# One layer of a hybrid decoder on one core: the last down projection by thirds of tokens with the final LayerNorm between its steps, the copy of x made later, the latents read back from another queue

## The chip, the cores and the metric

The kernel runs on one core of a Trainium2 chip. The metric is the device time of one execution in microseconds (us), the median over several runs. TensorE does the matrix products, VectorE and ScalarE the elementwise work and the reads of PSUM, GpSimd further elementwise work and the issue of some transfers, SyncE only issues transfers.

## What is computed

1024 prompt tokens and 8 x 4 sample tokens (T = 1056 in all) pass one layer. Cut to what matters here:

```python
z = x @ w_in + b_in                      # GLU | q latent 384 | kv latent 256 | rope key 64 | gates
u = causal_dwconv(a * sigmoid(g));  y_conv = silu(layer_norm(u)) @ w_conv_out
c_kv = rms_norm(z_kv);  q = rms_norm(z_q) @ w_uq;  o = attention(q, c_kv, rope(z_kr))
mix = (sigmoid(gA) * y_conv + sigmoid(gB) * (o @ w_uv @ w_mla_out)) @ w_mix_out
x1 = layer_norm(alpha * x + mix)
h = causal_dwconv(x1 @ w_up);  f = (silu(hg) * hv) @ w_down        # D_FF = 2816
y = layer_norm(alpha * x1 + f) * g2 + b2
```

Besides y the kernel returns the new latents, the last rows of both convolutions (the state rows) and, of the sample group, the old convolution rows moved on by four.

## The kernel before

**Layout.** Channels lie on the 128 partitions and tokens along the free axis, so that a tile is 128 channels x 1056 tokens, held in three thirds of 352 columns (`CH`). All products are made in float32 precision out of parts: `w = whi + wlo`, `x = xh + xl`, and each 128 x 128 block of weights takes three matmuls per third (`product`, L2006). ScalarE makes the high part `whi` of each block of weights (`hi`, L680), GpSimd the low part `wlo` (`lo`, L1244); two raw buffers (`RAW`) are filled by SyncE's transfers and each is released by `lo`. Two accumulators in PSUM, `psa` and `psb` (the buffers `psx[0]` and `psx[1]`, of three banks each), take turns, and the semaphores `free[0]` and `free[1]` count their reads; `pst` has two more banks. Everything is ordered by hand: each engine has its own list of instructions, and semaphores tie the lists together.

**Start.** Nine tiles of 128 tokens (the ninth has 32) are loaded as rows, turned over on TensorE (L2032), and read from PSUM three or four times: ScalarE writes `xh` (L688), VectorE `xl` (L1388), the sum over channels `stat` (L1390) and a copy of x, `xst` (L1393), which GpSimd sends to DRAM as `xt_d` (L1238). The copy has two buffers. Then come the turned tables of vectors (L2036 to L2042), the column sums of x (L2020) and the turned state rows (L2054), and only then the first of 32 products with `w_in` (`in_products`).

**Latents.** The latents z are made at the end of the first stage, `kv0 kv1 kr q0 q1 q2`, and go to DRAM as `z_d` from ScalarE's queue. ScalarE then makes the last two swish tiles (L803, L806), of which VectorE takes the low part `sl` (L1497), which the product `ya0` waits for tile by tile. After the last `z_d` is out, ScalarE issues in this order the read of all six tiles into `zbuf` (L839), of the gates `gab[0]` and `gab[1]` (L841) and of the rope table `cs` (L842), waits for `zbuf`, and squares five tiles (L845). TensorE's order is `ya0`, `ya1` (products with `w_conv_out`), the column sums `skv` (two tiles) and `sq` (three), `ya2` to `ya7`. VectorE multiplies each `ya` by its gate (`merge_a`, L1510), which frees the accumulator, and inverts the roots of the sums (L1516, L1519).

**FFN and end.** Eleven groups of two 128-row blocks of the inner width run over the up product, the convolution and the down product; each down product of a group has eight output tiles of 1056 tokens, 18 matmuls each (L2546), and VectorE adds each to `res` (L1924). After the last group's eight tiles TensorE turns the state rows (L2572, 11 x 4 transposes), ScalarE copies them (L1215) and issues nine transfers (L1217, L1220), and then the final LayerNorm goes over nine tiles of tokens:

```python
for t in range(9):
    y_stats(t)        # L1971 two bn_stats from PSUM, L1975 aggregate, L1977 1/root, L1980 -mean/root
    if t:
        y_gain(t - 1) # L1986 times g2, after ScalarE's scaling of the tile (L1228)
y_gain(8)
```

GpSimd adds `b2` (L1375) and SyncE sends the rows out (L659); after the last, SyncE issues the copy of the old state rows from DRAM to DRAM (L662). The tile of turned `res` has two places in PSUM, so that TensorE (L2581) waits for ScalarE's read of the tile before the last.

## Time and profile before

| what | value |
|---|---|
| median of 3 runs | 2242.74 us (2235.79 to 2242.78) |
| the profiled execution, its own time | 2257.73 us |
| its span, first to last instruction | 2255.9 us |
| TensorE busy (matmul) | 2111.7 us, 94% |
| VectorE / ScalarE / GpSimd busy | 57% / 30% / 24% |
| mean granted TensorE clock | 0.97 of full speed |

The table is the page of the profiled execution. Times in the rows below count from the start of its span. "Idle before" of an instruction, in square brackets, is what its engine waited and for whom. The profiled execution is 15.0 us longer than the median of the runs.

### The profile page before, as it was taken

Reading aid. Unit: us, or ns where it says so; the run is one execution under the profiler, and the core shown is the slowest. Engines: PE = TensorE matmul, PEld = TensorE weight load, DVE = VectorE, ACT = ScalarE, POOL = GpSimd, SP = SyncE. Lnnn points to the kernel's source line nnn. Section 1 sums busy time; section 2 is a strip of 40 time slices with the busy share of each in tenths; the row PEclk is TensorE's granted clock in tenths of the full one; section 3 lists DMA queues with packets and bytes.
Section 4 is the critical chain, followed back from the end, with each engine's and each line's share of the span. In section 5 each row is a group of like instructions: output and inputs, shape, how many; then the busy total and the mean of one; then the engine's idle time right before and its main releaser. Section 6 shows DMA issues by size and latency. Waiting matters only on the chain.

```text
span 2255.9 us, 34989 instructions
## 1 busy us (share of the span) xinstructions
PE 2111.7 (94%) x13793; PEld 1998.2 (89%) x13793; DVE 1279.5 (57%) x1748; ACT 666.7 (30%) x1107; POOL 535.6 (24%) x281
## 2 busy tenths in 40 slices
PE   5999999998989999979988999999999999999993
PEld 4999999997979888866657999899999999999992
DVE  5799999943546666634333324855445454454545
ACT  2222222243224444433332112522222122222212
POOL 2213343302100000033320134522222222222213
PEclk9999999999989999979997999999999999999995
DMA  7222232215310000046542442111111111111102
GB/s 234 77 87 82 85 113 85 87 46 196 125 41 13 12 23 12 19 163 234 190 178 95 143 108 89 31 54 46 40 47 38 47 41 53 46 37 52 45 25 99
DMA packets 163557, 182.78 MB, mean 81 GB/s; under 512 B 19838, under 2 KB 136376, under 8 KB 159303
## 3 DMA queue, kind: packets, MB, share of 16 engines
q1 hardware_dynamic: 144101, 102.36, 15.3%
q0 software_dynamic: 8368, 46.27, 5.4%
q10 hardware_dynamic: 10979, 32.68, 3.8%
q8 instruction: 71, 1.16, 0.2%
q14 instruction: 38, 0.30, 0.0%
HBM read 150.21 MB, written 31.93 MB: 81 GB/s over the span
## 4 chain that ended last, share of the span: by engine, by line
PE 70%; issue 13%; DVE 8%; POOL 3%; ACT 2%; DMA 2%; ACTq 1%; POOLq 0%; DVEq 0%; SPq 0%
PE psa L2006 21%; PE psb L2006 20%; PE psb L2160 5%; PE psa L2160 4%; PE psa L2546 4%; PE psb L2546 4%; POOL wlo L1363 3%; PE psb L2386 1%; PE pst L2365 1%; PE psa L2333 1%; PE psb L2333 1%; PE pst L2230 1%; DVE ptl L1612 1%; DMA gab<-ga_d 1%; DMA xt_d<-xst 1%
## 5 line engine op out<-in xcount | busy, mean ns | idle before, releaser
L1363 POOL TENSOR_TENSOR wlo<-wraw,whi 128x1024 fp32r<-128x1024 f32 x64 | 173.1, 2718 | 565.1 <-ACT whi L1167 565.1
L1444 DVE SCALAR_TENSOR_TENSOR pst<-g_ext,wtap,pst 128x512 f32<-128x512 f32 x464 | 306.9, 750 | 0.0
L1244 POOL TENSOR_TENSOR wlo<-wraw,whi 128x1024 fp32r<-128x1024 f32 x64 | 154.1, 2416 | 446.5 <-ACT whi L680 303.8
L1892 DVE TENSOR_SCALAR hg<-ueg,fwv,vec 128x1024 f32<-128x1024 f32 x22 | 19.3, 875 | 239.7 <-ACT ueg L1192 232.1
L2006 PE MATMUL psa<-x1h,whi 128*128 128x352 f32 x504 | 109.9, 326 | 3.5 <-POOL wlo L1363 2.0
L2006 PE MATMUL psa<-x1l,whi 128*128 128x352 f32 x504 | 109.1, 325 | 0.0
L2006 PE MATMUL psa<-x1h,wlo 128*128 128x352 f32 x504 | 109.0, 324 | 0.0
L2006 PE MATMUL psb<-x1h,whi 128*128 128x352 f32 x504 | 109.0, 324 | 0.0
L2006 PE MATMUL psb<-x1h,wlo 128*128 128x352 f32 x504 | 108.6, 323 | 0.0
L2006 PE MATMUL psb<-x1l,whi 128*128 128x352 f32 x504 | 108.5, 323 | 0.0
L1895 DVE SCALAR_TENSOR_TENSOR hg<-ueg,fwv,hg 128x1024 f32<-128x1024 f32 x44 | 97.0, 2204 | 5.7 <-DVE hg L1895 0.2
L2006 PE MATMUL psa<-xh,whi 128*128 128x352 f32 x456 | 98.8, 325 | 1.1 <-ACT stat L771 1.1
L2006 PE MATMUL psa<-xh,wlo 128*128 128x352 f32 x456 | 98.3, 323 | 0.0
L2006 PE MATMUL psa<-xl,whi 128*128 128x352 f32 x456 | 98.2, 323 | 0.0
L2006 PE MATMUL psb<-xh,whi 128*128 128x352 f32 x432 | 93.5, 324 | 1.5 <-POOL wlo L1244 1.5
L1292 POOL TENSOR_TENSOR wlo<-wraw,whi 128x1024 fp32r<-128x1024 f32 (+1 forms) x16 | 25.3, 1606 | 292.9 <-ACT whi L862 292.9
L2006 PE MATMUL psb<-xh,wlo 128*128 128x352 f32 x432 | 93.1, 323 | 0.0
L2006 PE MATMUL psb<-xl,whi 128*128 128x352 f32 x432 | 93.0, 323 | 0.0
L1192 ACT ACTIVATE ueg<-psa 128x1056 f32<-128x1056 f32 x22 | 23.2, 1054 | 229.3 <-PE psa L2006 222.8
L2006 PEld LDWEIGHTS psa<-x1h,whi 128*128 128x128 f32 x504 | 86.4, 190 | 4.1 <-issue 4.1
L2006 PEld LDWEIGHTS psa<-x1h,wlo 128*128 128x128 f32 x504 | 86.9, 189 | 0.0
L2006 PEld LDWEIGHTS psb<-x1h,wlo 128*128 128x128 f32 x504 | 86.5, 188 | 0.0
(472 smaller groups left out, 5450.8 us busy)
## 6 DMA issues: line engine op xcount, KB each, us to landing
wraw<-in_w_up SPq DMA_DIRECT2D x44, 512.0 KB, 3.8
wraw<-in_w_in SPq DMA_DIRECT2D x37, 512.0 KB, 3.8
wraw<-in_w_down SPq DMA_DIRECT2D x22, 512.0 KB, 3.5
gb_d<-stg ACTq DMA_DIRECT2D x8, 528.0 KB, 2.6
ga_d<-stg ACTq DMA_DIRECT2D x8, 528.0 KB, 3.8
gab<-ga_d ACTq DMA_DIRECT2D x8, 528.0 KB, 5.0
ma_d<-stg ACTq DMA_DIRECT2D x8, 528.0 KB, 2.9
tmp<-gb_d SPq DMA_DIRECT2D x8, 528.0 KB, 3.7
```

The costliest lines, as they stand in the source:

```text
L1192: nc.scalar.activation(split(ue[v][:, FW - 1:]), acc(v), ACT.Copy).then_inc(free[v], 1)
L1244: nc.gpsimd.tensor_tensor(wlo[:, n % HL, :], wraw[:, n % RAW, :], whi[:, n % HL, :].bitcast(F32), ALU.subtract).then_inc(lo_done, 1)
L1292: nc.gpsimd.tensor_tensor(wlo[:, n % HL, 0:w], wraw[:, v, 0:w], whi[:, n % HL, 0:w].bitcast(F32), ALU.subtract).then_inc(lo_done, 1)
L1363: nc.gpsimd.tensor_tensor(wlo[:, (ns + 2) % HL, :], wraw[:, (ns + 2) % RAW, :], whi[:, (ns + 2) % HL, :].bitcast(F32), ALU.subtract).then_ ...
L1444: half[x] = link(nc.vector.scalar_tensor_tensor(out=dst, in0=src, scalar=tap(k_), in1=pst[:, x, :], op0=ALU.mult, op1=ALU.add))
L1612: nc.vector.tensor_tensor(ptl[:, 4 * g:4 * g + nb, cols], pst[:, (cum(q) + g) % 2, 0:nb * P].rearrange("p (k n) -> p k n", n=P), pth[:, 4 ...
L1895: nc.vector.scalar_tensor_tensor(out=h, in0=src, scalar=tap(k), in1=h, op0=ALU.mult, op1=ALU.add).then_inc(h_chain, 1)
L2006: last = nc.tensor.matmul(out[:, c, 0:CH], w[:, k, :], x[:, k, c * CH:(c + 1) * CH], start=(k == 0 and x is hi_x and w is wh), stop=(k == ...
L2160: r = nc.tensor.matmul(out, w, x, start=first and k == 0, stop=last and k == len(steps) - 1)
L2230: last = nc.tensor.transpose(pst[:, (cum(q) + g) % 2, (k % 4) * P:(k % 4 + 1) * P], pbuf[q % 3][:, k * P:(k + 1) * P], ident[:, :])
L2333: last = nc.tensor.transpose(dst[:, k, v * P:(v + 1) * P], cb[j][:, 4 * g + v, k * P:(k + 1) * P], ident[:, :])
L2546: last = nc.tensor.matmul(psx[q][:, c, 0:CH], w[:, k, cols], x[:, k, c * CH:(c + 1) * CH], start=k == 0 and w is wh and x is fh[p_], stop= ...
```

## The change

**Start.** The copy `xst` and its transfers go. GpSimd later makes each of the eight channel tiles of x again as `xh + xl` (`x_tile`) and sends it to `xt_d`, three after each group of four products. The first product is put ahead of the tables, the column sums and the state rows (`start_tables`), and the first block of weights is loaded ahead of the last x rows.

**Latents.** The read-back of `z_d`, `gab` and `cs` is issued by SyncE, in another order and in more pieces; `q2` is read from PSUM before the last two swish tiles; `ya2` goes ahead of the column sums; VectorE adds the squares first, so that each column sum takes one tile.

**End.** The last group's down product goes third by third (24 steps of six matmuls, four places in PSUM), the nine tiles of the LayerNorm are put between its steps and behind them, with four places in PSUM, GpSimd multiplies tiles 0, 2, 4 and 6 by `g2` itself, and the state rows go to the end, with one transfer for the sample rows instead of eight.

```diff
         for k, name in enumerate(("kv0", "kv1", "kr", "q0", "q1", "q2", "ya0", "ya1",
-                                  "skv", "sq", "ya2", "ya3", "ya4", "ya5", "ya6", "ya7")):
+                                  "ya2", "skv", "sq", "ya3", "ya4", "ya5", "ya6", "ya7")):
...
+        LAST_DN = 6 * (NG - 1)
+        ROWS_BY_GPSIMD = (0, 2, 4, 6)
+        YB = "ABABACDBC"
...
+        def y_half(t, n, h):
+            b = YB[t]
+            if b == "A":
+                return pst[0:n, h, :]
+            if b == "B":
+                return psx[h][0:n, 2, :]
+            return psx["CD".index(b)][0:n, h, :]
...
+        def last_acc(i):
+            return psx[i % 2][:, i // 2 % 2, 0:CH]
...
+                if t == 8:
+                    load(0, w_in_v[:, :, 0:P])
                 sp.wait_ge(x_hi, t - 3)
...
-            with sp.Fori(0, MT // 2) as i:
+            load(N1C, w_co_v[:, :, 0:P])
+            load(N1C + 1, w_co_v[:, :, P:2 * P])
+            sp.wait_ge(w_used, N1C + HL)
+            sp.wait_ge(stg_out[0], 16 * (MT + 4))
+            sp.dma_start(gab[0][:, :], ga_d[0]).then_inc(ga_in[0], 16)
+            sp.wait_ge(stg_out[1], 16 * (MT + 3))
+            sp.dma_start(zbuf[:, 0:5, :], z_d[0:5].rearrange("k p n -> p k n")).then_inc(z_in, 16)
+            sp.wait_ge(stg_out[1], 16 * (MT + 4))
+            sp.dma_start(gab[1][:, :], ga_d[1]).then_inc(ga_in[1], 16)
+            sp.dma_start(zbuf[:, 5, :], z_d[5]).then_inc(z_in, 16)
+            sp.dma_start(cs[:, :], A["c_rope"]).then_inc(cs_in, 16)
+            with sp.Fori(1, MT // 2) as i:
...
-            read_z("q2", 5, 1, V_Q + 2)
-
-
-            act.wait_ge(w_used, N1C + HL)
-            for j in range(2):
-                act.wait_ge(stg_out[j], 16 * (MT + 4))
-            act.dma_start(zbuf[:, :, :], z_d.rearrange("k p n -> p k n")).then_inc(z_in, 16)
-            for j in range(2):
-                act.dma_start(gab[j][:, :], ga_d[j]).then_inc(ga_in[j], 16)
-            act.dma_start(cs[:, :], A["c_rope"]).then_inc(cs_in, 16)
-            act.wait_ge(z_in, 16)
-            for k in range(5):
-                nc.scalar.activation(sqb[:, k, :], zbuf[:, k if k < 2 else k + 1, :], ACT.Square).then_inc(rms_sq, 1)
+                    read_z("q2", 5, 1, V_Q + 2)
+
...
             after_ya(0)
+            act.wait_ge(z_in, 32)
+            for k in range(5):
+                nc.scalar.activation(sqb[:, k, :], zbuf[:, k if k < 2 else k + 1, :], ACT.Square).then_inc(rms_sq, 1)
             after_ya(1)
+            after_ya(2)
             stat_read("skv", 2, rk[:, :], 1.0 / KL, RMS_EPS)
             stat_read("sq", 3, rq[:, :], 1.0 / QL, RMS_EPS)
-            after_ya(2)
             after_ya(3)
...
+            def state_copy(*rs):
+                for r in rs:
+                    act.wait_ge(kf_t, r + 1)
+                    nc.scalar.activation(fout[:, r * 512:(r + 1) * 512], pst[0:FK, r % 2, :], ACT.Copy).then_inc(kf_r, 1)
...
-                nc.scalar.activation(yrow[t % 4][0:n, :], psx[j][0:n, 0:2, :].rearrange("p b n -> p (b n)"),
-                                     ACT.Identity, scale=sd[j][0:n, 1:2], bias=mv[j][0:n, 0:1]).then_inc(y_n, 1)
+                for h in range(2):
+                    ins = nc.scalar.activation(yrow[t % 4][0:n, h * 512:(h + 1) * 512], y_half(t, n, h),
+                                               ACT.Identity, scale=sd[j][0:n, 1:2], bias=mv[j][0:n, 0:1])
+                ins.then_inc(y_n, 1)
+                state_copy(*{5: (0, 1), 6: (2, 3), 7: (4, 5, 6), 8: (7, 8, 9, 10)}.get(t, ()))
+            act.wait_ge(kf_r, FT // 2)
+            act.dma_start(O["ffn_p"][0, 0], fout[0:FW - 1, :]).then_inc(ffn_out, 16)
+            act.dma_start(O["ffn_s"][0].rearrange("b t c -> (b t) c"), fout[FW - 1:, :]).then_inc(ffn_out, 16)
...
-                n = P if t < 8 else NS
-                pool.wait_ge(free[t % 2], t // 2 + 2)
-                pool.dma_start(xt_d[:, :, t * P:t * P + n].rearrange("m p n -> p m n"), xst[t % 2][:, :, 0:n]
-                               ).then_inc(xt_out[t % 2], 16)
...
+            def x_tile(k):
+                if k >= 2:
+                    pool.wait_ge(xt_out[k % 2], 16 * (k // 2))
+                nc.gpsimd.tensor_tensor(tmp[k % 2][:, :], xh[:, k, :].bitcast(F32), xl[:, k, :].bitcast(F32), ALU.add
+                                        ).then_inc(x_sum, 1)
+                pool.wait_ge(x_sum, k + 1)
+                pool.dma_start(xt_d[k], tmp[k % 2][:, :]).then_inc(xt_out[k % 2], 16)
...
                 lo(4 * m)
                 lo(4 * m + 1)
+                if m == 0:
+                    pool.wait_ge(free[0], 6)
+                    pool.wait_ge(free[1], 5)
...
                 if m >= CSUM:
                     for k in ((0, 1) if m == CSUM else (m - 2,)):
                         centre(k)
-                lo(4 * m + 2)
-                lo(4 * m + 3)
+                for t in range(2):
+                    lo(4 * m + 2 + t)
+                    if m < CSUM:
+                        for k in range(3 * m, min(MT, 3 * m + 3)):
+                            if (k > 3 * m) == (t == 1):
+                                x_tile(k)
                 if m >= CSUM:
                     add_squares(max(1, m - 2))
...
-                pool.wait_ge(y_g, t + 1)
+                if t in ROWS_BY_GPSIMD:
+                    k = ROWS_BY_GPSIMD.index(t) + 1
+                    pool.wait_ge(y_n, t + 1)
+                    nc.gpsimd.tensor_tensor(yrow[t % 4][0:n, :], yrow[t % 4][0:n, :], g2[0:n, :], ALU.mult).then_inc(y_gp, 1)
+                    pool.wait_ge(y_gp, k)
+                else:
+                    pool.wait_ge(y_g, t - sum(v < t for v in ROWS_BY_GPSIMD) + 1)
                 nc.gpsimd.tensor_tensor(yrow[t % 4][0:n, :], yrow[t % 4][0:n, :], b2[0:n, :], ALU.add).then_inc(y_b, 1)
...
-                nc.vector.reduce_sum(stat[:, t * P:t * P + n], src.rearrange("p k n -> p n k"), axis=AX.X)
-                if t >= 2:
-                    dve.wait_ge(xt_out[t % 2], 16 * (t // 2))
-                nc.vector.tensor_copy(xst[t % 2][:, :, 0:n], src).then_inc(free[t % 2], 1)
+                nc.vector.reduce_sum(stat[:, t * P:t * P + n], src.rearrange("p k n -> p n k"), axis=AX.X
+                                     ).then_inc(free[t % 2], 1)
...
-            dve.wait_ge(xt_out[0], 16 * 5)
-            dve.wait_ge(xt_out[1], 16 * 4)
...
+            for a, b in ((0, 1), (2, 3)):
+                dve.wait_ge(rms_sq, b + 1)
+                nc.vector.tensor_tensor(sqb[:, a, :], sqb[:, a, :], sqb[:, b, :], ALU.add).then_inc(rms_add, 1)
+            dve.wait_ge(rms_sq, 5)
+            dve.wait_ge(rms_add, 2)
+            nc.vector.tensor_tensor(sqb[:, 2, :], sqb[:, 2, :], sqb[:, 4, :], ALU.add).then_inc(rms_add, 1)
+            merge_a(2)
             ready("skv")
             nc.vector.reciprocal(rk[:, :], rk[:, :]).then_inc(rms_c, 1)
-            merge_a(2)
...
+            def last_add(*steps):
+                for i in steps:
+                    c, m = divmod(i, MT)
+                    dve.wait_ge(dn_done, LAST_DN + i + 1)
+                    nc.vector.tensor_tensor(res[:, m, part3(c)], res[:, m, part3(c)], last_acc(i), ALU.add).then_inc(dl_add, 1)
...
-            for t in range(9):
-                y_stats(t)
-                if t:
-                    y_gain(t - 1)
+            last_add(*range(10))
+            y_stats(0)
+            last_add(10, 11)
+            y_scale(0)
+            last_add(12)
+            y_stats(1)
+            last_add(13)
+            y_scale(1)
+            last_add(14, 15, 16)
+            y_gain(1)
+            last_add(17)
+            y_stats(2)
+            last_add(18)
+            y_scale(2)
+            last_add(19, 20)
+            y_stats(3)
+            last_add(21)
+            y_scale(3)
+            last_add(22)
+            y_gain(3)
+            y_stats(4)
+            last_add(23)
+            y_scale(4)
+            y_stats(5)
+            y_stats(6)
+            y_scale(5)
+            y_scale(6)
+            y_gain(5)
+            y_stats(7)
+            y_scale(7)
+            y_stats(8)
+            y_scale(8)
+            y_gain(7)
             y_gain(8)
 
 
...
             pe.wait_ge(free[1], 5)
-            def in_products(m, past):
+            def start_tables():
...
+            def in_products(m, past, between=None):
                 for t in range(4):
+                    if between is not None and t == 1:
+                        between()
                     pe.wait_ge(lo_done, 4 * m + (RAW + t + 1))
                     pe.wait_ge(free[t % 2], 2 * m + (U1A[t % 2] + t // 2 + 1 + (0 if t % 2 else past)))
                     product(t, t % 2, xh, xl)
 
-            with pe.Fori(0, CSUM) as m:
+            in_products(0, 0, start_tables)
+            with pe.Fori(1, CSUM) as m:
...
-            pe.wait_ge(rms_sq, 2)
-            column_sums(ready("skv"), [sqb[:, k, :] for k in range(2)])
-            pe.wait_ge(rms_sq, 5)
-            column_sums(ready("sq"), [sqb[:, k, :] for k in range(2, 5)])
+            weighed(N1C + 2, "ya2", sh, sl)
+            pe.wait_ge(rms_add, 1)
+            column_sums(ready("skv"), [sqb[:, 0, :]])
+            pe.wait_ge(rms_add, 3)
+            column_sums(ready("sq"), [sqb[:, 2, :]])
...
+            def y_tile(t):
+                n = P if t < 8 else NS
+                pe.wait_ge(dl_add, MT * (y_third(t) + 1))
+                if y_last(t) is not None:
+                    pe.wait_ge(y_n, y_last(t) + 1)
                 for m in range(MT):
-                    last = nc.tensor.transpose(psx[j][0:n, m // 4, (m % 4) * P:(m % 4 + 1) * P],
+                    last = nc.tensor.transpose(y_half(t, n, m // 4)[:, (m % 4) * P:(m % 4 + 1) * P],
                                                res[:, m, t * P:t * P + n], ident[:, :])
                 last.then_inc(y_t, 1)
...
+            for i in range(3 * MT):
+                c, m = divmod(i, MT)
+                n, ns = blk("last", DOWN1 if m >= MT // 2 else DOWN0)
+                wh, wl = (x[:, ns % HL, :].rearrange("p (k c) -> p k c", k=2) for x in (whi, wlo))
+                cols = slice(m % 4 * P, (m % 4 + 1) * P)
+                if i in (0, MT // 2):
+                    pe.wait_ge(lo_done, n + (RAW + 1))
+                if i >= 4:
+                    pe.wait_ge(dl_add, i - 3)
+                for k in range(2):
+                    if i == 0:
+                        pe.wait_ge(fl_done, j2 + (k + 2))
+                    for w, x in ((wh, fh[0]), (wh, fl[0]), (wl, fh[0])):
+                        last = nc.tensor.matmul(last_acc(i), w[:, k, cols], x[:, k, part3(c)],
+                                                start=k == 0 and w is wh and x is fh[0], stop=k == 1 and w is wl)
+                last.then_inc(dn_done, 1)
+                if i in (9, 12, 17, 20, 22):
+                    y_tile((9, 12, 17, 20, 22).index(i))
+            y_tile(5)
+            y_tile(6)
+            pe.wait_ge(se_set, 2 * FT)
+            pe.wait_ge(y_n, 5)
+            y_tile(7)
+            state_rows_out(0, 1)
+            y_tile(8)
+            state_rows_out(*range(2, FT // 2))
```

How the instructions stand. First TensorE at the start (`xrow` are the x rows, `vrow`, `crow`, `frow` the tables, `strows` the state rows), before:

```order
L2032 MATMUL psa<-ident,xrow_92 128x32 x8
L2036 MATMUL pst<-ident,vrow 128x127
L2039 MATMUL pst<-ident,crow 128x124 x2
L2042 MATMUL pst<-ident,frow 128x66 x2
L2020 MATMUL psb<-stat,ones 128x352 x3
L2054 MATMUL pst<-ident,strows 128x120 x16
```

and now:

```order
L2113 MATMUL psa<-ident,xrow_92 128x32 x8
L2087 MATMUL psa<-xh,whi 128x352 x3
...
L2121 MATMUL pst<-ident,vrow 128x127
L2124 MATMUL pst<-ident,crow 128x124 x2
L2127 MATMUL pst<-ident,frow 128x66 x2
L2101 MATMUL psb<-stat,ones 128x352 x3
L2139 MATMUL pst<-ident,strows 128x120 x16
L2087 MATMUL psb<-xh,whi 128x352 x3
```

A whole product of 72 matmuls stands between the last x tile and the tables. Next ScalarE around the last latents, before:

```order
L831 DMA out_conv_s<-krow 4x1024 x8
L803 ACTIVATE tmp_78<-u,vec 128x1056
L806 ACTIVATE sh<-tmp_78 128x1056
L803 ACTIVATE tmp_79<-u,vec 128x1056
L806 ACTIVATE sh<-tmp_79 128x1056
...
L839 DMA zbuf<-z_d 128x6x1056
L841 DMA gab_103<-ga_d 128x1056
L841 DMA gab_104<-ga_d 128x1056
L842 DMA cs<-in_c_rope 128x1056
L845 ACTIVATE sqb<-zbuf 128x1056 x5
```

and SyncE's queue now:

```order
L530 DMA wraw<-in_w_conv_out 128x8x128 x2
L584 DMA gab_101<-ga_d 128x1056
L586 DMA zbuf<-z_d 128x5x1056
L588 DMA gab_102<-ga_d 128x1056
L589 DMA zbuf<-z_d 128x1056
L590 DMA cs<-in_c_rope 128x1056
L591 UNCONDITIONAL_BRANCH
L591 ISA
L594 ISA
L594 DMA wraw<-in_w_conv_out 128x8x128
```

The read-back left ScalarE's queue, and the weights of `ya2`, the last row, now stand behind it. Last, VectorE behind the last step of the down product, now (`g_207` is g2; `pst`, `psa` and `psb` hold turned tiles):

```order
L2014 TENSOR_TENSOR res<-res,psb 128x352
L2029 RECIPROCAL sd_213<-sd_213 128x1
L2032 SCALAR_TENSOR_TENSOR mv_211<-mv_211,sd_213 128x1
L2020 BN_STATS bst_210<-psa 128x6 x2
L2024 BN_AGGR mv_212<-bst_210 128x2
L2020 BN_STATS bst_209<-psb 128x6 x2
L2024 BN_AGGR mv_211<-bst_209 128x2
L2029 RECIPROCAL sd_214<-sd_214 128x1
L2032 SCALAR_TENSOR_TENSOR mv_212<-mv_212,sd_214 128x1
```

The statistics of tiles 5 and 6 follow the last addition at once; those of tiles 0 to 4 stand between the additions ahead of it.

## Rows read from the trace of the kernel before

**Rows 1.** The page, part 4: the chain that ended last, by engine.

```profile
PE 70%; issue 13%; DVE 8%; POOL 3%; ACT 2%; DMA 2%; ACTq 1%; POOLq 0%; DVEq 0%; SPq 0%
```

**Rows 2.** Timeline of the start: start us, us, engine, line, operation, [idle before].

```profile
7.81 1.23 DVE L1388 TENSOR_TENSOR xl<-psa,xh 128x1024 fp32r<-128x1024 f32 x1 [6.80 <-ACT xh L688]
...
11.45 1.94 PE L2032 MATMUL psa<-ident,xrow 128*128 128x128 f32 x8 [2.07 <-DVE xst L1393]
...
13.42 1.02 ACT L688 ACTIVATE xh<-psa 128x1024 fp32r<-128x1024 f32 x1 [2.98 <-PE psa L2032]
...
38.48 1.23 DVE L1393 COPY xst<-psb 128x1024 f32<-128x1024 f32 x1 [3.50 <-DMA xt_d<-xst]
```

**Rows 3.** Chain of waits, start: start us, us, what.

```profile
40.75 3.60 PE psb L2020 x6
...
47.70 11.68 PE psa L2006 x72
```

**Rows 4.** Timeline of GpSimd in the first stage.

```profile
85.47 2.40 POOL L1244 TENSOR_TENSOR wlo<-wraw,whi 128x1024 fp32r<-128x1024 f32 x1 [6.75 <-ACT whi L734]
```

**Rows 5.** Chain of waits around the latents.

```profile
524.94 15.63 DMA gab<-ga_d
...
542.06 5.57 PE psa L2020 x12
547.63 5.33 PE psb L2020 x18
552.95 11.61 PE psa L2006 x72
564.56 11.65 PE psb L2006 x72
```

**Rows 6.** Timeline of ScalarE and TensorE around the latents.

```profile
515.07 1.27 ACT L803 ACTIVATE tmp<-u,vec 128x1056 f32<-128x1056 f32 x1 [3.55 <-DVE u L1494]
...
520.59 1.13 ACT L779 ACTIVATE stg<-psb,vec 128x1056 f32<-128x1056 f32 x1
...
539.34 3.03 ACT L845 ACTIVATE sqb<-zbuf 128x1056 f32<-128x1056 f32 x3 [17.63 <-DMA zbuf<-z_d]
...
511.50 0.74 PE L2006 MATMUL psa<-sh,whi 128*128 128x352 f32 x3 [1.16 <-POOL wlo L1244]
```

**Rows 7.** Windows: busy PE, PEld, DVE, ACT, POOL, clock, DMA share, GB/s.

```profile
530.00:540.00 10.00, 5.26 (x33) 4.96 (x31) 0.00 (x0) 0.66 (x1) 0.00 (x0) 0.94 0.95 386
```

**Rows 8.** Chain of waits at the end of the last down product.

```profile
2191.94 2.91 PE psb L2546 x18
```

**Rows 9.** Timelines of ScalarE, VectorE and GpSimd in the final LayerNorm.

```profile
2202.68 9.43 ACTq L1220 DMA_DIRECT2D out_ffn_s<-fout  x8
...
2220.81 1.28 DVE L1971 BATCH_NORM_STATS2 bst<-psb 128x6 f32<-128x512 f32 x2
...
2222.80 0.53 DVE L1980 SCALAR_TENSOR_TENSOR mv<-mv,sd 128x1 f32<-128x1 f32 x1
2223.25 1.21 DVE L1986 TENSOR_TENSOR yrow<-yrow,g 128x1024 f32<-128x1024 f32 x1
...
2220.97 2.35 POOL L1375 TENSOR_TENSOR yrow<-yrow,b 128x1024 f32<-128x1024 f32 x1 [1.23 <-DVE yrow L1986]
...
2245.90 2.33 POOL L1375 TENSOR_TENSOR yrow<-yrow,b 32x1024 f32<-32x1024 f32 x1 [1.15 <-DVE yrow L1986]
```

**Rows 10.** Timelines of VectorE and GpSimd, one moment of the down product.

```profile
2171.58 1.25 DVE L1924 TENSOR_TENSOR res<-res,psb 128x1056 f32<-128x1056 f32 x1 [0.29 <-PE psb L2546]
...
2171.03 2.52 POOL L1363 TENSOR_TENSOR wlo<-wraw,whi 128x1024 fp32r<-128x1024 f32 x1 [16.87 <-ACT whi L1167]
```

**Rows 11.** Line L1802: durations of its instructions (min/median/max, ns) at two widths.

```profile
L1802 DVE SCALAR_TENSOR_TENSOR res<-stg,psb x6: 508/888/1255, 1336.8 to 1410.1; 128x1056 f32<-128x1056 f32 x3, 128x352 f32<-128x352 f32 x3
```

**Rows 12.** Timeline of TensorE: a turned tile at full and at half clock.

```profile
2201.54 1.04 PE L2581 MATMUL psa<-ident,res 128*128 128x128 f32 x8
...
2221.04 1.97 PE L2581 MATMUL psa<-ident,res 128*128 128x128 f32 x8 [1.68 <-ACT yrow L1228]
```

125 lines of the change are left out of this document (59 added, 66 removed).

## The prediction

> **What bounds the kernel now.** I read the page first: TensorE carries 70% of the chain that ended last, "issue" and all other engines and transfers the rest [rows 1]. The change touches no product, so it can only gain where TensorE is not the bound. The chain of waits shows three such places: the start up to the first product at 47.70 [rows 3], the column sums between `ya1` and `ya2` [rows 5], and all that follows the last down product, which ends at 2194.85 [rows 8]. For each I went to the timelines to see which wait ends last. In rows 2 the reader is to see that VectorE stands in the cycle of each x tile with three reads, the third of which also waits for a transfer; in rows 5 and 6 that one read from DRAM, issued late, holds TensorE; in rows 9 that after the last matmul VectorE's list is the chain, and that GpSimd holds it up.
>
> **Start.** A tile's buffer is turned (1.94), read by ScalarE (1.02) and by VectorE. With the copy gone VectorE takes two reads of 1.23, which overlap by 0.10, so 2.26. With some 0.2 for three hand-overs a buffer takes 5.4, and with two buffers a tile takes 2.7 us [rows 2]. VectorE's first tile starts at 7.81, the eighth ends at 7.81 + 7 x 2.7 + 2.26 = 29.0 and the short ninth by 29.7. The first weights, loaded before the last x rows, are split on ScalarE right behind the last x tile (by 29.1) and on GpSimd in 2.40 [rows 4]: the first product starts at 31.5 instead of 47.70. What stood ahead of it now stands between the first and the second product: the turned tables (less than the 1.04 of a turned tile [rows 12]; I take 1.0), the column sums, and the state rows with their hand-overs, 47.70 - (40.75 + 3.60) = 3.35. The six column sums took 3.60 at the start [rows 3], but eighteen took 5.33 at full clock [rows 5], or 1.8 for six. The granted-clock row says 1.0 at both, yet the pace of the first is that of the half clock (1.2 against 2.4 GHz), after an idle TensorE. Now the product comes first after the idle time and pays the 1.8, and the column sums no longer do. The second product starts at 31.5 + 11.68 + 1.8 + 1.0 + 1.8 + 3.35 = 51.1, before at 59.38: **8.3 us**. From below: if x rows arrive no faster than before, a tile takes 3.4 us, as the three reads do now, and 2.7 are left. From above: without the tables, 10.
>
> **The copy of x later.** Each of eight tiles costs GpSimd one sum of 2.5 us (2.40 [rows 4] by 1056/1024) and an issue of about 1. GpSimd is busy 2.40 in each product of 11.65 [rows 3, 4], so it has 37 idle of 46.6 us in four products, against 10.5 for three tiles. I cost it at nothing; the cover is this idle time. If it went, the low parts of the weights would be late, and TensorE behind them. The Trainium skill (SBUF — State Buffer, section SBUF: two separate sides) has a rule against this place: a transfer issued by GpSimd has its descriptors written by GpSimd, which some VectorE operations lock out, and VectorE is never idle in this stage. By it the issues stretch; nothing in the rows above prices that.
>
> **Latents.** The read of `q2` goes ahead of the last two swish tiles. Its weights' high part (1.05), the read (1.13) and the issue (0.36) move the swish from 515.07 to 517.6 [rows 6]. Tile 7's low part is then there at 523.6 (two swishes and copies at 2.4 a tile, then one VectorE step of 1.25 [rows 10]), while `ya0`, started at 511.50 [rows 6], wants it after seven of eight parts, at 521.7: `ya0` and `ya1` end 1.9 later, at 537.1. The read-back was issued just before 524.94 and the first gate landed at 540.6 [rows 5]. Now `gab[0]` and five tiles of z are issued at about 513 and the rest at 520. All of it and the weights of `ya2`, which are queued behind, are 5.4 MB. At 386 GB/s [rows 7] from 515 that is over at 529; at the pace of the old read (3.8 MB in 15.63 us [rows 5]) at 537. The weights need 1.05 and 2.40 more, so `ya2` starts at 537.1 with no wait, or at 541 at the worst. I take no wait, since most bytes are then ahead of the late part. The squares (1.06 each on ScalarE, three in 3.03 [rows 6]) and their sums lie beside `ya2`. `ya2` ends at 548.8, `skv` with one tile takes 1.8, and `ya3` needs its buffer read: two issues, a table load and the read, of which 2.7 stick out, an estimate between the one read of 1.1 and twice as much again. So `ya3` starts at 553.3 instead of 564.56 [rows 5]: **11.2 us**, 7 if the weights are late, and 5 if TensorE then also starts at half clock. The reciprocals, which follow `skv`, move behind it but have 60 us to the attention.
>
> The Trainium skill (DMA: Bandwidth & Descriptors, section Queues, rings and completion order) says that each DMA engine takes the descriptors of one queue in order and goes round between queues. By this rule the move from ScalarE's queue to SyncE's puts the weights of `ya2` behind all of the read-back, where before they would have passed it, and the sum would take the late value. Rows 5 fit it in so far as `gab` landed only behind z.
>
> **End.** The 24 steps hold the same matmuls, 8 x 2.91 = 23.3 [rows 8]. Five turned tiles between them cost 5 x 1.04 = 5.2 [rows 12], so the last step ends at 2200.1. An addition of 352 columns is 0.51 long, about 0.44 back to back [rows 11], and a step 0.97, so VectorE keeps up. Rows 9 show what follows: the small `mv` step at 2222.80 takes 0.53 and ends at 2223.33, just when GpSimd's addition ends (2220.97 + 2.35). `bn_stats`, which reads PSUM, ran beside the same addition at its 1.28, and an addition with one operand in PSUM ran beside GpSimd at its 1.25 [rows 10]. So a VectorE step with both operands in SBUF and a GpSimd step exclude each other. After 2201.0, when they start to alternate without a pause, there remain eight GpSimd steps of 2.34 (18.7), four gains of 1.16 (4.6) and `mv` steps (0.5), 23.8 in all, and two pauses that I find by laying the lists side by side: 1.4 for ScalarE's scaling of tile 4, and 3.0 where ScalarE copies two state tiles before the root of tile 6. GpSimd ends at 2229.2 instead of 2248.23 [rows 9]: **19.0 us**. What follows it, 7.7 to the end of the span, stays. The state rows' issue (9.43 [rows 9]) leaves the path; their last copy is over near 2227 and their transfer has the 7.7 and 2 more. From above: with no exclusion at all the same lists end at 2224.8 (23.4 gained). From below: if additions with an operand in PSUM were excluded too, at 2235.8 (12.4 gained).
>
> **Sum.** 8.3 + 11.2 + 19.0 = 38.5 us. The profiled execution took 2257.73 and would take 2219.2. It stands 15.0 above the median of the runs, and I know no reason why that part should change, so the median goes from 2242.74 to **2204**. A measurement of this kernel tells 0.3%, or 6.7 us, from no change.
>
> **Rivals.**
> - *The weights of `ya2` come late.* For it: they are the last of 5.4 MB in one queue. Against it: 8 us of room at 386 GB/s. 2204 + 6 = 2210. Chance 0.12.
> - *The exclusion is wider*, and the additions wait for GpSimd too: 2204 + 6.6 = 2211. Rows 10 speak against it, but the two are close in only one place. Chance 0.10.
> - *The exclusion is looser*, the end at 2224.8: 2200. Rows 9 speak against it. Chance 0.10.
> - *The start does not gain what it says*, since the x rows' transfers set the pace: 2204 + 5.6 = 2210. For it: TensorE's second tile already waits for rows. Against it: the copies' 4 MB leave the same DMA engines. Chance 0.06.
> - *Slower: the x tiles hold up the weights.* Each x tile but two waits for an earlier tile's write. If every tile had to wait out 15.63, the longest landing in the rows [rows 5], it would take 18.1 us, against a room of 37/3 = 12.3, and TensorE would lose 5.8 eight times, 47 us: 2251. It decides from a wait of some 10 us on; the writes have only one buffer each, but the stage has spare bandwidth. The rule on descriptors above would work in this direction. Chance 0.02.
>
> My forecast, 0.60, has 2196 to 2212 as its own range (3 either way at the start, 4 at the latents, 6 at the end, and runs that differ by 7). The range of 8 in 10 takes in the four near rivals: 2194 to 2217. Faster by over 0.3% hold all cases but the last, less a little for a mistake common to all: 0.95; within 0.3%: 0.03; slower: 0.02.
>
> **What would show it.** Start: the first product near 31.5, the second near 51, x tiles every 2.7. Latents: no wait ahead of `ya2`, and `ya3` near 545 in the new count (553.3 less 8.3). End: last down step 28.5 after the first; `mv` and gain steps that end when GpSimd's end; GpSimd's last step some 29 behind the last down step. I would be wrong if TensorE waited for `wlo` in the first stage, for additions between the down steps, or if the chain at the end ran over the state rows' transfer.

## The result and the profile after

| | kernel before | changed kernel |
|---|---|---|
| median of 4 runs | 2240.47 us | **2202.12 us** (2198.99 to 2203.72) |
| ratio to before, 95% interval | 1 | **0.9823** (0.9803 to 0.9842) |
| the profiled execution, its own time | 2257.73 us | 2203.72 us |
| span | 2255.9 us | 2201.8 us |

The changed kernel takes 38.4 us less. The prediction of 2204 is 2 us off. The two profiled executions differ by 54.0 us, 16 more than the medians; the first experiment is about those 16.

The page of the changed kernel begins its part 4, the chain that ended last, with this line, which answers to [rows 1]:

```profile
PE 85%; DVE 6%; ACT 3%; issue 2%; POOL 1%; DMA 1%; ACTq 0%; SPq 0%; POOLq 0%; DVEq 0%
```

TensorE now has 85% of the chain. Timeline of TensorE at the start, now (answers to [rows 2, 3]):

```profile
25.82 1.03 PE L2113 MATMUL psa<-ident,xrow 32*128 32x32 f32 x8 [1.20 <-DVE stat L1437]
30.90 1.22 PE L2087 MATMUL psa<-xh,whi 128*128 128x352 f32 x3 [4.04 <-POOL wlo L1268]
...
33.67 1.08 PE L2087 MATMUL psa<-xh,whi 128*128 128x352 f32 x3
...
35.84 0.65 PE L2087 MATMUL psa<-xh,whi 128*128 128x352 f32 x3
...
45.03 1.99 PE L2101 MATMUL psb<-stat,ones 128*128 128x352 f32 x6
...
50.14 0.74 PE L2087 MATMUL psb<-xh,whi 128*128 128x352 f32 x3
```

The first product starts at 30.90 and pays the half clock: a group of three of its matmuls takes 1.08, later ones 0.65. The second starts at 50.14 here and at 50.38 in the chain of waits, in which it stood at 59.38 before (47.70 + 11.68 [rows 3]). Next SyncE's queue at the latents, with the column sums and `ya3` on TensorE (answers to [rows 5, 6]):

```profile
502.20 0.34 SPq L584 DMA_DIRECT2D gab<-ga_d  x1
502.59 0.44 SPq L586 DMA_DIRECT2D zbuf<-z_d  x1
514.57 0.33 SPq L588 DMA_DIRECT2D gab<-ga_d  x1
517.65 9.53 SPq L594 DMA_DIRECT2D wraw<-in_w_conv_out  x3
```

```profile
526.58 0.75 PE L2087 MATMUL psa<-sh,whi 128*128 128x352 f32 x3 [0.24 <-POOL wlo L1268]
...
538.34 1.94 PE L2101 MATMUL psb<-sqb,ones 128*128 128x352 f32 x6
...
543.17 0.72 PE L2087 MATMUL psb<-sh,whi 128*128 128x352 f32 x3 [1.11 <-ACT rk L826]
```

`ya2` starts with a wait of 0.24 us for the low part of its weights, and `ya3` starts at 543.17 in place of 564.56. Last, the start of the last down product on TensorE, and the timelines of GpSimd and VectorE near the end (answer to [rows 8, 9]):

```profile
2132.68 0.65 PE L2632 MATMUL psb<-fh,wlo 128*128 128x352 f32 x3
2134.92 0.40 PE L2684 MATMUL psa<-fh,whi 128*128 128x352 f32 x1 [1.59 <-issue]
```

```profile
2169.95 2.35 POOL L1418 TENSOR_TENSOR yrow<-yrow,g 128x1024 f32<-128x1024 f32 x1 [1.58 <-ACT yrow L1253]
2172.37 2.34 POOL L1422 TENSOR_TENSOR yrow<-yrow,b 128x1024 f32<-128x1024 f32 x1
...
2178.85 2.34 POOL L1422 TENSOR_TENSOR yrow<-yrow,b 128x1024 f32<-128x1024 f32 x1 [4.14 <-DVE yrow L2038]
...
2187.13 2.34 POOL L1422 TENSOR_TENSOR yrow<-yrow,b 128x1024 f32<-128x1024 f32 x1 [1.22 <-DVE yrow L2038]
2190.63 2.33 POOL L1422 TENSOR_TENSOR yrow<-yrow,b 32x1024 f32<-32x1024 f32 x1 [1.15 <-DVE yrow L2038]
```

```profile
2171.55 1.30 DVE L2020 BATCH_NORM_STATS2 bst<-psb 128x6 f32<-128x512 f32 x2 [0.17 <-PE psb L2655]
2172.88 0.21 DVE L2024 BATCH_NORM_AGGREGATE mv<-bst 128x2 f32<-128x12 f32 x1
2173.01 0.11 DVE L2029 RECIPROCAL sd<-sd 128x1 f32<-128x1 f32 x1
2173.15 1.58 DVE L2032 SCALAR_TENSOR_TENSOR mv<-mv,sd 128x1 f32<-128x1 f32 x1
...
2187.42 3.13 DVE L2038 TENSOR_TENSOR yrow<-yrow,g 32x1024 f32<-32x1024 f32 x1 [0.37 <-ACT yrow L1253]
```

While GpSimd multiplies and adds, from 2169.95 to 2174.71, VectorE's statistics, aggregate and reciprocal run at their usual length; the `mv` step, which has two operands in SBUF and one element for each partition, takes 1.58 and ends at 2174.73, just when GpSimd does. The gain of the last tile takes 3.13, to 2190.55; GpSimd's addition beside it ends at 2189.47, and the usual gain is 1.1 to 1.2 long. GpSimd ends at 2192.96, 58.0 us after the first down step.

### The profile page after: what moved, and what is told of

It is laid out like the page before. It is cut to its first block, busy times and chain, and to the rows that moved or that the text cites. A ratio compares the mean times of both kernels' runs of the same rounds, so it can differ in the third digit from the quotient of the medians.

```text
span 2201.8 us, 34966 instructions
## 1 busy us (share of the span) xinstructions
PE 2092.7 (95%) x13775; PEld 1988.1 (90%) x13775; DVE 1276.7 (58%) x1754; ACT 668.9 (30%) x1116; POOL 561.4 (25%) x292
## 4 chain that ended last, share of the span: by engine, by line
PE 85%; DVE 6%; ACT 3%; issue 2%; POOL 1%; DMA 1%; ACTq 0%; SPq 0%; POOLq 0%; DVEq 0%
PE psa L2087 27%; PE psb L2087 26%; PE psb L2632 5%; PE psa L2632 5%; PE psb L2246 5%; PE psa L2246 5%; PE psb L2472 1%; PE pst L2451 1%; PE psa L2419 1%; PE psb L2419 1%; PE pst L2316 1%; DVE ptl L1661 1%; PE pst L2454 1%; DVE pbuf L1653 1%; PE psb L2202 1%
```

## Experiments

Three groups of four runs (e, f and g). The runs of a group share a chip and the runs of the kernel before; the chip is another one in each group. All are the kernel before or the changed kernel with one edit. Tails are counted from the first step of the last down product to the end of the span, since the stages ahead of it scatter by some us from one execution to the next.

### The kernel before, profiled again

> The kernel before, unchanged, profiled once more. In the first profiled execution the samples' stage, from its third-last read of a chunk's scores at 1003.85 to 1157.54, took 153.7 us, and in the changed kernel's profile the same stretch took 136.1 (982.70 to 1118.82), 17.6 less, though the change touches nothing there. Theory A (scatter of one execution): this profile shows some 136 to 140 us in that stretch, a span near 2238, and the two traces then differ by about 38, as the medians do. Rival B (the change makes that stage faster, for instance by where its transfers fall): this profile shows 150 us or more again.

Ratio 0.9992 (0.9979 to 1.0004), span 2238.8. ScalarE's reads of `ct` that bound the stretch, first in the profile of the section ahead of the prediction, then in this one:

```profile
1003.85 0.60 ACT L1019 ACTIVATE ct<-psa 128x512 f32<-128x512 f32 x1 [11.10 <-PE psa L2345]
1157.54 0.60 ACT L1019 ACTIVATE ct<-psa 128x512 f32<-128x512 f32 x1 [9.94 <-remote]
```

```profile
1003.97 0.60 ACT L1019 ACTIVATE ct<-psa 128x512 f32<-128x512 f32 x1 [11.07 <-PE psa L2345]
1140.70 0.60 ACT L1019 ACTIVATE ct<-psa 128x512 f32<-128x512 f32 x1 [6.79 <-PE psa L2333]
```

153.7 us against 136.7, and 136.1 in the changed kernel. Rival B falls: the excess of the first profile over its median lies in this stretch and is not the kernel's. But it is no scatter of one execution either, as Theory A has it. In the second group the stretch took 153.7 to 154.0 in all four profiles (984.50 to 1138.19 in f0), and all executions of both kernels were longer (2257.16 for before, 2222.21 for the changed kernel, ratio 0.9834). In the eight profiles of the other two groups, on two other chips, it took 135.6 to 136.7. So the length goes with the group, that is with the chip or its hour; which of them, and on which chip the first profile was taken, is not on record.

This second profile of the kernel before also shows `ya3` sooner than the first one, which had it at 564.56. The gate's transfer and `ya3` in the chain of waits:

```profile
525.13 12.63 DMA gab<-ga_d
...
561.55 11.65 PE psb L2006 x72
```

The landing of this gate took 15.63 in the first profile, and 12.63, 13.87 and 14.02 in e0, e1 and e3, which have the old latents.

### One part alone

The edits are the change's own diff, as the section on the change divides it: e1 has what stands there under Start, e2 what stands under Latents, e3 what stands under End, each alone in the kernel before.

> The kernel before with the start of the change alone (no copy of x, first product ahead of tables, sums and state rows, x tiles by GpSimd later). Theory A (the parts add up and each is worth what its own stretch shows): second product at 50.4 in place of 59.38, 9.0 us less, 2231.5 at a median before of 2240.5; GpSimd's x tiles cost nothing. Rival B (the x tiles hold up weights a little in the first stage, which the changed kernel's trace shows as a wait of 4.0 us once): the gain at the end of the first stage is under 7, 2234 or more.

> The kernel before with the latents' part alone (read-back by SyncE in pieces, q2 read before the last swish tiles, ya2 ahead of the column sums, squares added by VectorE). Theory A: 12.4 us less, as the changed kernel's trace shows from the first stage's end to ya3, 2228. Rival B (part of the 12.4 needs the start's part, since the last weights or writes before it come at another time): 7 or less, 2233 or more.

> The kernel before with the end alone (last down product by thirds, LayerNorm inside it, state rows at the very end, four gains on GpSimd). Theory A: the end takes 66.9 us from the first down step to the end of the span in place of 84.35, 17.5 us less, less the wait of 1.6 in front of the first step, so 16 to 17.5: 2223 to 2225. Rival B (the forecast's 19.0 holds and this profile's slower pieces were scatter): 2221.

| run | ratio (95%) | of 2237.53 us | in its trace |
|---|---|---|---|
| e1 | 0.9963 (0.9951 to 0.9975) | -8.3 | the rest of the first stage 7.9 us earlier |
| e2 | 0.9939 (0.9918 to 0.9960) | -13.6 | `ya3` at 553.64; in the kernel before 564.56 (first profile) and 561.55 (e0): 10.9 or 7.9 |
| e3 | 0.9920 (0.9897 to 0.9944) | -17.9 | tail 67.4 behind a wait of 1.5, before 84.5: 15.6 |

The three sum to 39.8 us, and the whole change has 0.0177 of 2240, 39.7. The parts add up, within intervals of 3 to 5 us either way for each part.

- e1: Theory A, though at 8 and not at 9.0. The interval (5.6 to 11.0) would also hold Rival B's "under 7"; the trace's 7.9 speaks against it.
- e2: the interval (9.0 to 18.3) leaves out Rival B's 7. Theory A's 12.4 was read off the slow first profile. Counted from the second product to `ya3`, e2 took 493.9 and e0 501.9, so that its trace has 8.0. The runs measured 5.6 more than that; the rest lies in later stages, which the edit does not touch and which differ by some us from trace to trace.
- e3: the interval (12.5 to 23.0) holds both Theory A's 16 to 17.5 and Rival B's 19. The traces decide: the tail of e0 is 84.6, and this one 67.4 behind 1.5.

### The end of the program

> The changed kernel once more, as the ground for the three others of this group: 2201 to 2203 at a median before of 2240. Its tail from the first last-down step to the end of the span again 66.9 us, of it 8.8 behind GpSimd's last step; if one of these was scatter of one execution (the mv steps of 0.96 to 1.58, the issue of the last copy of 2.04), it shows here.

Ratio 0.9834 (0.9812 to 0.9855); tail 67.0, GpSimd's last step 58.1 after the first down step, `mv` steps again of 0.97, 1.16 and 1.59, and the last copy's issue 2.04. None of it was scatter.

```diff
+            sp.dma_start(O["conv_s"][0, :, 0:HALO - NT, :], A["state_conv"][0, :, NT:, :]).then_inc(out_s, 16)
             sp.wait_ge(h_chain, 12 * FT + 12)
...
-            sp.dma_start(O["conv_s"][0, :, 0:HALO - NT, :], A["state_conv"][0, :, NT:, :]).then_inc(out_s, 16)
```

> The changed kernel with the copy of the old state rows from DRAM to DRAM issued ahead of the rows of g2 and b2, not behind the last rows of y. Theory A (this copy alone is what stands between GpSimd's last step and the end, 7.1 us of packets in the trace): the end then is the landing of the sample rows of y or of the state rows of the FFN, some 4 to 5 us behind GpSimd's last step in place of 8.8, so 4 us less, 2198. Rival B (the end of a program costs the same whatever the last transfer is): no difference. Rival C (the copy then stands in the way of weights): no gain, and TensorE waits near it.

Ratio 0.9821 (0.9797 to 0.9845), 3 us under the f0 kernel, and inside its interval. The trace is sharper: tail 64.2, GpSimd's last step again at 58.0, and 6.2 behind it in place of 8.9. Rival B falls, and Rival C too: from 2100 to 2185 TensorE waits for nothing but the 1.6 ahead of the first down step, as in f0. Theory A holds for the copy, with 2.8 in place of 4, but not for what comes next. The last rows of y landed at 2216.99, 3.8 behind GpSimd's last step, and SyncE was done at 2217.5; yet the span ends at 2219.42. What still runs is the DRAIN that ends each engine's list, here SyncE's and GpSimd's (duration in ns three times, first and last start):

```profile
L65 SPq DRAIN  x1: 13/13/13, 2217.4 to 2217.4; - x1
...
L65 POOLq DRAIN  x1: 8345/8345/8345, 2210.8 to 2210.8; - x1
```

GpSimd's begins with its last step (2210.85) and ends at 2219.19, 6.0 behind that step. It ends 5.4 or 6.0 behind it in all fourteen traces, and lay under the copy in those where the copy is last.

```diff
-        ROWS_BY_GPSIMD = (0, 2, 4, 6)
+        ROWS_BY_GPSIMD = ()
...
+            y_gain(0)
```

(and `y_gain` of tiles 2, 4 and 6 likewise, each ahead of the statistics of a later tile; GpSimd's branch for its own gains is then never taken)

> The changed kernel with all nine gains on VectorE, none on GpSimd; GpSimd only adds b2. Theory A (a VectorE step with both operands in SBUF and a GpSimd step never run at once, so what counts is the sum of both): four steps of 2.34 go and four of 1.16 come, and laid side by side the lists end within 0.2 us of the changed kernel: no difference, 0 plus or minus 1.5. Rival B (no exclusion; the gains were moved to GpSimd because VectorE is the longer list): 2 us slower by the same lists, up to 4.6 slower if all four gains lie on VectorE's path.

Ratio 0.9846 (0.9824 to 0.9868), tail 67.4, GpSimd's last step 58.1 after the first down step. Its list has nine steps in place of thirteen and ends at the same place:

```profile
2185.75 2.35 POOL L1422 TENSOR_TENSOR yrow<-yrow,b 128x1024 f32<-128x1024 f32 x1 [2.84 <-DVE yrow L2038]
...
2198.74 2.34 POOL L1422 TENSOR_TENSOR yrow<-yrow,b 128x1024 f32<-128x1024 f32 x1 [4.13 <-DVE yrow L2038]
```

Theory A, by the trace. The runs alone can't decide: f2 is 2.7 us above f0 by the ratios, inside both intervals, and Rival B had 2 to 4.6. In the trace the tail is 0.4 longer. That GpSimd makes four of the gains is worth next to nothing: a gain there takes 2.34 of a time that VectorE can't use for its own gains.

```diff
-                    ins = nc.scalar.activation(yrow[t % 4][0:n, h * 512:(h + 1) * 512], y_half(t, n, h),
-                                               ACT.Identity, scale=sd[j][0:n, 1:2], bias=mv[j][0:n, 0:1])
...
+                nc.scalar.activation(yrow[t % 4][0:n, :], yrow[t % 4][0:n, :], ACT.Copy, scale=sd[t % 4][0:n, 1:2]).then_inc(y_g, 1)
...
-                nc.vector.tensor_tensor(yrow[t % 4][0:n, :], yrow[t % 4][0:n, :], g2[0:n, :], ALU.mult).then_inc(y_g, 1)
...
+                    ins = nc.vector.scalar_tensor_tensor(
+                        out=yrow[t % 4][0:n, h * 512:(h + 1) * 512], in0=y_half(t, n, h), scalar=mv[j][0:n, 0:1],
+                        in1=g2[0:n, h * 512:(h + 1) * 512], op0=ALU.subtract, op1=ALU.mult)
```

(the `mv` step goes, and so do GpSimd's gains, with `pool.wait_ge(y_g, t + 1)` for all tiles; VectorE's order is written anew: statistics, gain and reciprocal of a tile together)

> The changed kernel with the LayerNorm's steps cut otherwise: VectorE makes (x - mean) times g2 straight from PSUM, in two halves, ScalarE multiplies by 1/root in SBUF, GpSimd only adds b2; the small mv step goes. No VectorE step with two operands in SBUF is left. Theory A (only those are locked out by GpSimd): every half gain takes 0.7 whatever GpSimd does, GpSimd's last step ends at 2184.5 in place of 2193.0 when counted from the same first down step, 8.5 us less, 2193.5; 6 to 10. Rival B (GpSimd locks out every VectorE step, or those that write SBUF): the half gains show 1.2 to 2.4 beside GpSimd's steps, and the gain is under 4.

Ratio 0.9798 (0.9774 to 0.9821), 8.1 us under f0 in its group; the tail is 58.2, 8.8 shorter. VectorE and GpSimd in its timeline:

```profile
2189.38 0.21 DVE L2016 BATCH_NORM_AGGREGATE mv<-bst 128x2 f32<-128x12 f32 x1
2189.63 1.41 DVE L2028 SCALAR_TENSOR_TENSOR yrow<-psa,mv,g 128x512 f32<-128x512 f32 x2
2190.95 0.15 DVE L2021 RECIPROCAL sd<-sd 128x1 f32<-128x1 f32 x1
```

```profile
2189.42 2.35 POOL L1413 TENSOR_TENSOR yrow<-yrow,b 128x1024 f32<-128x1024 f32 x1 [1.29 <-ACT yrow L1252]
```

Two half gains from PSUM took 1.41 together in the middle of a GpSimd step, and each of the eighteen took 0.73 to 0.75. GpSimd ended 47.3 us after the first down step, 10.8 sooner where Theory A had 8.5; 2 of that were lost again behind it, where the last copy and the state rows' transfer then ran together (10.9 in place of 8.9). Theory A; Rival B falls, since no gain was stretched.

```diff
-            return psx[i % 2][:, i // 2 % 2, 0:CH]
+            return psx[i // 2 % 2][:, i % 2, 0:CH]
...
-            for q in range(2):
-                pe.wait_ge(free[q], acc5("last", DOWN0, q) + 1)
...
+                if i in (0, 2):
+                    pe.wait_ge(free[i // 2], acc5("last", DOWN0, i // 2) + 1)
```

> The changed kernel, but the first two steps of the last down product both write psa and the next two psb, and TensorE waits for psb only before the third. In the changed kernel's trace TensorE stood 1.59 us before the first step, until VectorE's addition from psb of the step before had ended. Theory A: that wait goes whole, all behind it comes 1.5 us earlier, 0.9993 of the changed kernel, 1.5 us less. Rival B (VectorE's list, which then has the same additions to make, sets the pace): the wait goes, but additions or the first turned tile come no earlier, and the end moves by under 0.5 us.

Ratio 0.9855 (0.9831 to 0.9879): the timing cannot resolve 1.5 us, and leans the other way. In the trace the wait is gone and the tail is as long as ever (66.9 from 2130.44, GpSimd's last step 57.9 after it):

```profile
2129.95 0.65 PE L2632 MATMUL psb<-fh,wlo 128*128 128x352 f32 x3
2130.44 0.32 PE L2684 MATMUL psa<-fh,whi 128*128 128x352 f32 x1
```

So the trace has Theory A, with the tail 1.5 us earlier and no longer, and the runs leave it open.

### The latents

```diff
+            load(N1C + 2, w_co_v[:, :, 2 * P:3 * P])
             sp.wait_ge(stg_out[1], 16 * (MT + 4))
             sp.dma_start(gab[1][:, :], ga_d[1]).then_inc(ga_in[1], 16)
```

> The changed kernel with the weights of ya2 issued ahead of the second gate, the last tile of z and the rope table. In the changed kernel they were issued at 517.65, landed 5.3 later, and TensorE waited 0.24 for their low part. Theory A (the weights had come just in time, and what is in front of them in SyncE's queue and its waits is what made them late): they are issued near 503 and used at 512, the wait of 0.24 goes, nothing else: 0 to 0.3 us less, no difference. Rival B (the read-back is what must come early): the gate and the last z tile land later, the squares or the merge hold up skv, and it gets 1 us or more slower.

Ratio 0.9856 (0.9830 to 0.9881), no difference that can be told. SyncE's queue and ScalarE's read of these weights:

```profile
504.04 0.44 SPq L586 DMA_DIRECT2D zbuf<-z_d  x1
504.52 0.52 SPq L530 DMA_DIRECT2D wraw<-in_w_conv_out  x1
```

```profile
518.32 1.06 ACT L716 ACTIVATE whi<-wraw 128x1024 fp32r<-128x1024 f32 x1 [4.90 <-DMA wraw<-in_w_conv_out]
```

`ya2`'s wait went, as Theory A says, but not as it says it. The weights, issued at 504.52, landed 13.8 us later, at 518.3 and not in time for 512: behind the five tiles of z in the same queue, whose read took 12.8 and ended at 516.8. The first packet of the weights left at 515.24. In the same stretch of the changed kernel a write of one z tile from ScalarE's queue, issued at 506.49, landed in 8.1, before 2.66: its packets stood behind the last of the state rows in that queue until 510.44, and then ran to 514.2 while the read's still ran, to 515.2. A transfer in the same queue waits for nearly all of the read; one in another queue is slowed but gets through. That is what the Trainium skill says (DMA: Bandwidth & Descriptors, section Queues, rings and completion order).

### The start

```diff
-                nc.gpsimd.tensor_tensor(tmp[k % 2][:, :], xh[:, k, :].bitcast(F32), xl[:, k, :].bitcast(F32), ALU.add
-                                        ).then_inc(x_sum, 1)
-                pool.wait_ge(x_sum, k + 1)
+                for v in range(3):
+                    nc.gpsimd.tensor_tensor(tmp[k % 2][:, :], xh[:, k, :].bitcast(F32), xl[:, k, :].bitcast(F32), ALU.add
+                                            ).then_inc(x_sum, 1)
+                    pool.wait_ge(x_sum, 3 * k + v + 1)
```

> The changed kernel with every sum of an x tile made three times, 16 more GpSimd steps of 2.46 in the first twelve products, 39 us of work. Theory A (GpSimd's idle time, 37 us of every four products, covers it): three tiles with their issues take some 25 us of it; no difference, and no new wait of TensorE for wlo. Rival B (the cover is smaller, since two of three tiles come between two low parts that TensorE wants 11.65 apart: 2.4 + 2 x (7.4 + 0.9) = 19 us in one product): TensorE waits some 5 to 8 us for wlo once per four products, 10 to 20 us slower in all.

Ratio 0.9842 (0.9814 to 0.9870), no difference. GpSimd's timeline:

```profile
66.47 8.47 POOL L1295 TENSOR_TENSOR tmp<-xh,xl 128x1056 f32<-128x1056 f32 x3
75.25 0.59 POOL L1298 DMA_DIRECT2D xt_d<-tmp  x1 [0.31 <-POOL tmp L1295]
75.85 7.59 POOL L1295 TENSOR_TENSOR tmp<-xh,xl 128x1056 f32<-128x1056 f32 x3
84.34 4.74 POOL L1268 TENSOR_TENSOR wlo<-wraw,whi 128x1024 fp32r<-128x1024 f32 x2
```

and the line of TensorE's waits that answers to it, first in the changed kernel, then here:

```profile
PE psa L2087 <- POOL wlo L1268: 5.4, 3, 4.0
```

```profile
PE psa L2088 <- POOL wlo L1268: 6.8, 4, 4.0
```

The figures are the sum, the number of waits and the longest, over the whole span. The longest, 4.0, is that of the first product. Of the 1.4 us more, 1.0 lies in the first stage (5.0 against 4.0 up to 500 us) and 0.4 at `ya2` (0.62 against 0.24). So 39 us of added work cost TensorE 1 us; Rival B's 10 to 20 are not there. The last row of GpSimd's timeline shows two low parts back to back: GpSimd had fallen behind by one and caught up. The issue of an x tile took 0.57 to 0.59 in seven of eight cases in the changed kernel and 0.77 in one, with VectorE busy throughout, and a hand-over of 0.3 stands ahead of it: 3.4 for a tile, as costed (3.5).

### All together

> The changed kernel with gains made from PSUM as before, the copy of the old state rows issued early, the accumulators' order of the first steps changed, the weights of ya2 first, and the turning and copying of the state rows spread over tiles 5 to 8. Theory A (the terms add up): from the first down step to the end of the span 54.3 us in place of 67.0, set by the FFN's state rows, whose transfer ends some 8 us behind its issue; with 0.24 at ya2 and 1.5 before the first step counted in the 54.3's start, 12 to 13 us less than the changed kernel, 0.977 of the kernel before. Rival B (the terms overlap: with the copy away and the rows of y sooner, VectorE, busy from the tenth step on, is the bound, and the earlier start of 1.5 us is lost): 10 to 11 less.

Ratio **0.9783** (0.9764 to 0.9803), 2190.85 at a median before of 2238.08; the changed kernel had 0.9823 and 0.9834 in its groups. Of the same group g1, g2 and g3, which are the changed kernel or within 1.5 us of it, have 0.9855, 0.9856 and 0.9842, so this one is 13 to 16 us less: Theory A and a little more, not Rival B's 10 to 11. Tail 53.5, from a first step without the wait: 13.5 and 1.5 under f0, 15.0 in all. The last step of GpSimd and the last issue:

```profile
2183.74 2.33 POOL L1415 TENSOR_TENSOR yrow<-yrow,b 32x1024 f32<-32x1024 f32 x1 [0.87 <-ACT yrow L1254]
2186.10 0.34 SPq L696 DMA_DIRECT2D out_y_s<-yrow  x1
```

This version beats both kernels. 6.2 us stand between GpSimd's end and the end of the span, and it is not the state rows that fill them, as expected: their packets end at 2190.0, the rows of y land at 2190.9, and GpSimd's DRAIN ends at 2192.1, 6.0 behind its last step, 0.2 ahead of the end of the span.

## Why the prediction was right, by its steps

**Start, 8.3 predicted.** 9.0 by the chain of waits, 8.3 by the runs of e1, 7.9 by its trace. Over all fourteen traces the second product starts at 59.4 in the mean with the old start (four) and at 51.1 with the new (ten): 8.3 again. The first product came at 30.90 for 31.5, and two x tiles every 5.5 for 5.4, so the rival of slow x rows falls. The half clock cost it 2.0 (the tables follow at 44.59, so it was 13.7 long, against 11.68) for 1.8, and the column sums took 1.84 for 1.8. The tables took 0.44 for the 1.0 that was taken.

**Copy later, nothing predicted.** Right, and with much room, as g3 shows. The Trainium skill's rule on descriptors (SBUF — State Buffer, section SBUF: two separate sides) did not bite here: the issues were not stretched. VectorE's work beside them was for the most part the convolution's steps, which read one operand from PSUM (76.8 us of the 101 from 54 to 155).

**Latents, 11.2 predicted.** `ya3` came 21.4 earlier, of which about 9 come from the start: 12.4 against the first profile. Most of what this has above 9 is that profile's own. From the start of the second product to the start of `ya3` it took 505.2; e0, e1 and e3, with the old latents too, took 501.9 to 502.5, and the ten traces with the new latents 492.9 to 495.2, 493.5 in the mean. That makes 8.7. The forecast place of the new `ya3` was right (545 predicted, 543.2 to 545.2 in the traces of the changed kernel and its variants); the old one, 564.56, was some 3 us late in the one trace that the prediction had, with the slow landing of the gate. The term was therefore too large by 2.5.

The rival of late weights (0.12) was closer than its chance said. Its "8 us of room" leaves out the 1.05 and 2.40 that the weights need after landing: 537.1 less 532.5 is 4.6. And the prediction let them wait only for bytes; in fact SyncE first stood until 514.57, waiting for the write of the last z tile, which landed in 8.1 us beside the read-back. The forecast of no wait failed by little: of the eight traces with this order, seven show a wait of 0.24 to 1.32 ahead of `ya2`, one none.

**End, 19.0 predicted.** 84.35 before (by the chain of waits; 84.5 by the timeline) against 66.9 and the wait of 1.6: 15.9. e3 has 15.6 by its trace and 17.9 by its runs. The exclusion was right to the operand: GpSimd's last step ended 58.0 after the first down step for the 57.65 of the lists, the two pauses were 1.6 for 1.4 and 3.0 for 3.0 (4.14 less a gain of 1.16), and f2 ended where the lists said. In f3, with no such step left, VectorE was no longer held. The wider exclusion (0.10) falls with it, since steps with an operand in PSUM kept their length, and the looser one (0.10) by the `mv` steps. The 24 steps with their five tiles took 27.6 for 28.5. Two small terms were missed:

- *The wait that the change adds before the first down step*, 1.6. Step one writes `psa`, but TensorE waits for both accumulators, and `psb` had just been filled. The prediction's working started the 24 steps where the old ones had started.
- *"What follows it, 7.7 to the end of the span, stays."* It was 8.8. The copy from DRAM to DRAM, the last in SyncE's queue, took 2.04 to issue for 0.85, and its first packet left that much later; its packets then took 4.9 as before. (The 7.1 us in f1's expectation are the packets of the last rows of y and of the copy together, 6.1 before.) f1 shows that 2.8 of the 8.8 go with the copy, and that GpSimd's DRAIN is the floor below it.

**Sum.** For 38.5 predicted the medians have 38.4, with an interval of 35.4 to 44.1 from the ratio, and the parts' runs 39.8. The traces place less: 8.3 + 8.7 + 15.9 = 32.9 over all of them, and 34.3 between e0 and the changed kernel, whose spans differ by 37.0. The rest lies in stages that the change does not touch. From `ya3` to the last down product, without the stretch above, they took 1448 to 1458 in the fourteen traces, 1455 in the mean of the four with the old latents and 1453 in that of the others, so no run says whether a part of it is the change's. So the mechanisms were right, two of the three terms were 2.5 to 3 us too large, and that the sum came within 0.1 us is luck.

"I know no reason why that part should change" failed for the profiled execution, not for the median: the first profile stood 15 us above the median by its slow stretch above all, 17.0 longer than in e0.

The slower rival, x tiles that hold up the weights, is refuted by g3: even three times the sums cost TensorE 1 us.

## What to carry to other kernels

Where VectorE and GpSimd share a list, count the GpSimd steps and the VectorE steps with both operands in SBUF as one engine's work; moving such a step between the two gained nothing here (f2), while reading one operand from PSUM took it out of the sum (f3). When a change reorders steps at a seam, look at the first wait behind the seam: buffers that used to alternate may be wanted all at once. Look at what the last queue entry is; a copy that depends on nothing does not belong there. And compare a part with more than one trace of the kernel before: here 3 us at the latents and 17 in the samples' stage were the first profile's own.
